# Seven chunk pairs of the token projections as Strassen products, interleaved with blocks of the pair before

## The reference

```python
h = rmsnorm(x, g_mix_pre[l])
proj = h @ w_in[l]                                   # (256, 2048) @ (2048, 7168)
cb, cc, cv, dq, dk, dv, xq = jnp.split(proj, IN_OFFSETS, axis=-1)
y_conv = short_conv_mixer(cb, cc, cv, conv_w[l]) @ w_conv_out[l]
y_diff = diff_attention(dq, dk, dv, ...) @ w_diff_out[l]
y_cross = memory_cross_attention(xq, rmsnorm(mem, g_mem[l]), w_mem_kv[l]) @ w_cross_out[l]
```

## Time and profile before

| | |
|---|---|
| median of 3 runs | 1637.32 us (1637.16 to 1637.5) |
| the profiled execution | 1637.66 us, span 1635.8 us |
| PE, PEld busy | 1624.0 us (99%), 1338.5 us (82%) |
| DVE, ACT busy | 1090.9 us (67%), 858.3 us (52%) |
| DMA | 346.75 MB, mean 212 GB/s |

### The profile page before, as it was taken

The page is one execution under the profiler, slowest core; times in us unless marked ns, Lnnn a source line. Parts: engine busy times, 40 slices in busy tenths (PEclk is TensorE's granted clock), DMA queues, the critical chain, the costliest instruction groups (busy, mean ns, idle before and its releaser), DMA issues.

```text
span 1635.8 us, 21990 instructions
## 1 busy us (share of the span) xinstructions
PE 1624.0 (99%) x7225; PEld 1338.5 (82%) x7225; DVE 1090.9 (67%) x1463; ACT 858.3 (52%) x1080; POOL 54.8 (3%) x117
## 2 busy tenths in 40 slices
PE   9999999999999999999999999999999999999998
PEld 7888888888888888888888888888888888877886
DVE  5664565655566566666665756777766777789886
ACT  6744444444444444444444656666666565555553
POOL 2500000000000000000000000000000000000000
PEclk9999999999999999999999999999999999999999
DMA  8877666777665766676666476777777767665564
GB/s 282 279 223 216 196 183 190 228 215 218 188 208 190 239 216 200 200 235 210 221 222 223 133 224 209 217 219 220 219 216 218 221 204 227 216 203 200 192 206 155
DMA packets 207787, 346.75 MB, mean 212 GB/s; under 512 B 28952, under 2 KB 52329, under 8 KB 207209
## 3 DMA queue, kind: packets, MB, share of 16 engines
q1 hardware_dynamic: 201033, 342.48, 67.2%
q0 software_dynamic: 2048, 2.10, 0.4%
q10 hardware_dynamic: 4640, 1.33, 0.3%
HBM read 318.02 MB, written 2.10 MB: 196 GB/s over the span
## 4 chain that ended last, share of the span: by engine, by line
PE 96%; DVE 2%; DMA 0%; ACT 0%; issue 0%; SPq 0%; POOL 0%; DVEq 0%; ACTq 0%; POOLq 0%
PE PS L1725 24%; PE PS L1727 24%; PE PS L1726 24%; PE PS L1973 3%; PE PS L1974 3%; PE PS L1972 3%; PE PS L1857 3%; PE PS L1859 3%; PE PS L1858 3%; PE PS L1957 1%; PE PS L1959 1%; PE PS L1958 1%; DVE w_lo L1586 1%; PE PS L1893 1%; PE PS L1895 1%; PE PS L1894 1%
## 5 line engine op out<-in xcount | busy, mean ns | idle before, releaser
L1112 DVE TENSOR_TENSOR w_lo<-raw,w_hi 128x1024 fp32r<-128x1024 f32 x479 | 583.1, 1224 | 453.6 <-ACT w_hi L676 452.4
L676 ACT ACTIVATE w_hi<-raw 128x1024 fp32r<-128x1024 f32 x479 | 504.9, 1059 | 496.4 <-PE PS L1727 431.3
L1725 PE MATMUL PS<-w_hi,hT_hi 128*128 128x512 f32 x1504 | 587.7, 391 | 0.0
L1727 PE MATMUL PS<-w_hi,hT_lo 128*128 128x512 f32 x1504 | 585.2, 389 | 0.0
L1726 PE MATMUL PS<-w_lo,hT_hi 128*128 128x512 f32 x1504 | 585.1, 389 | 0.0
L1725 PEld LDWEIGHTS PS<-w_hi,hT_hi 128*128 128x128 f32 x1504 | 282.4, 188 | 61.2 <-issue 2.7
L1727 PEld LDWEIGHTS PS<-w_hi,hT_lo 128*128 128x128 f32 x1504 | 282.4, 188 | 58.5
L1726 PEld LDWEIGHTS PS<-w_lo,hT_hi 128*128 128x128 f32 x1504 | 282.4, 188 | 58.3
L1586 DVE TENSOR_TENSOR w_lo<-raw,w_hi 128x1024 fp32r<-128x1024 f32 x81 | 98.1, 1221 | 28.1 <-ACT w_hi L1030 26.9
L1030 ACT ACTIVATE w_hi<-raw 128x1024 fp32r<-128x1024 f32 x81 | 84.8, 1057 | 59.8 <-PE PS L1974 38.2
L1972 PE MATMUL PS<-w_hi,act_hi 128*128 128x512 f32 x240 | 93.8, 391 | 1.9 <-DVE w_lo L1586 1.9
(11 more groups left out here) (243 smaller groups left out, 1637.7 us busy)
## 6 DMA issues: line engine op xcount, KB each, us to landing
raw<-in_w_up_dram SPq DMA_DIRECT2D x176, 512.0 KB, 4.0
raw<-in_w_in_dram SPq DMA_DIRECT2D x112, 512.0 KB, 4.2
raw<-in_w_gate_dram SPq DMA_DIRECT2D x96, 512.0 KB, 4.6
raw<-in_w_down_dram SPq DMA_DIRECT2D x88, 512.0 KB, 4.4
raw<-in_w_mem_kv_dram SPq DMA_DIRECT2D x32, 512.0 KB, 5.8
raw<-in_w_o_dram SPq DMA_DIRECT2D x32, 512.0 KB, 4.2
up_moved<-up_stage SPq DMA_DIRECT2D x352, 32.0 KB, 2.8
raw<-in_w_conv_out_dram SPq DMA_DIRECT2D x16, 512.0 KB, 3.7
```

The source lines that it names most:

```text
L676: nc.scalar.activation(w_hi[i % RING][:], raw[i % RING][:], ACT.Copy).then_inc(hi_ready, inc)
L1112: nc.vector.tensor_tensor(w_lo[i % RING][:], raw[i % RING][:], w_hi[i % RING][:].bitcast(F32), ALU.subtract).then_inc(lo_ready, inc)
L1725: nc.tensor.matmul(o, a_hi, b_hi, start=first, stop=False)
L1727: last = nc.tensor.matmul(o, a_lo, b_hi, start=False, stop=last_k)
```

## The change

For every even chunk c from 4 to 16 (`PAIRS`) the chunks c and c+1 form a pair. Their blocks 0 and 1 (the first four K tiles) are a matrix of four weight blocks: `b11` and `b21` of chunk c, `B12` and `B22` of chunk c+1. With the four token blocks (two token tiles by two pairs of K tiles) they are computed as seven products by Strassen's scheme (Winograd's form) in place of eight. A product is one weight operand by one token tile: 6 matmuls.

- A group has 11 units (`G_UNITS`), numbered 0 to 10 in the text: products are units 0, 2, 4, 5, 7, 8 and 10; units 1, 3, 6 and 9 are the blocks 4, 5, 6 and 7 of chunk c-1. After the group come blocks 2 to 7 of chunk c, then blocks 2 and 3 of chunk c+1, then the next group.
- Units take the place of blocks in the rings of `w_hi` and `w_lo` (4 deep). The raw ring carries only `b11`, `b21` and ordinary blocks; `B12` and `B22` are loaded into side buffers (`side_load`), where DVE also builds the four weight differences (`difference`, L1515, semaphore `p_sums`).
- Four sums of token blocks are made once (`token_sums`), with their own split `T_hi`, `T_lo`.
- Two partial results that several outputs share are carried by ACT copies (L978 from bank to bank, L987 into `side_q`, semaphore `p_seed`) and two DVE adds per group into PSUM (L1550, L1557, `p_folds`).
- The side work of the blocks that a group passes is called between its units (`after(k)`), and SP's small DMAs stand between other loads (`crossing`, `odd_squares`). An odd chunk uses banks 2 and 3 or 4 and 5 in turn.
- The later stages keep their instructions; their ring indices are rotated.

```diff
+    PAIRS = range(4, NP, 2)
+    G_UNITS = 11
+    N_BR = NP * CB + 3 * len(PAIRS)
+    RING_LOADS = NP * CB - 2 * len(PAIRS)
...
+        ODD = {1: (2, 3), 5: (4,), 7: (5,), 8: (6,), 9: (7,)}
+        THIRD = {1: (4,), 3: (5,), 6: (6,), 9: (7,)}
...
+        def p_passed(c, u):
+
+            if u == G_UNITS - 1:
+                return [(c, 0), (c, 1)]
+            return [(c - 1, i) for i in (THIRD if c == PAIRS[0] else ODD).get(u, ())]
...
+            for c in PAIRS:
+                proj_load(c, 0)
+                if c > PAIRS[0]:
+                    odd_squares(c - 3, 2)
+                proj_load(c - 1, 4)
+                crossing(c - 1, 4)
+                if c > PAIRS[0]:
+                    odd_squares(c - 3, 3)
+                proj_load(c - 1, 5)
+                crossing(c - 1, 5)
+                odd_squares(c - 2, 0)
+                proj_load(c, 1)
+                odd_squares(c - 2, 1)
+                proj_load(c - 1, 6)
+                odd_squares(c - 2, 2)
+                proj_load(c - 1, 7)
+                odd_squares(c - 2, 3)
+                for i in range(2, CB):
+                    proj_load(c, i)
+                    crossing(c, i)
+                    if i in (5, 6) and c + 2 in PAIRS:
+                        side_load(c + 2, i - 5)
+                for i in (2, 3):
+                    proj_load(c + 1, i)
+                    odd_squares(c - 1, i - 2)
...
+            def proj_group(c):      # ACT
+                proj_split(c, 0)
+                if g:
+                    after_projection(c - 2)
+                proj_split(c - 1, 4)
+                after(1)
+                proj_hi(u + 2, E, (p_sums, 4 * g + 1))
+                proj_split(c - 1, 5)
+                after(3)
+                act.wait_ge(block_done, u + 1)
+                nc.scalar.activation(p_bank(c)[:, 0, :], p_bank(c)[:, 1, :], ACT.Copy).then_inc(p_seed, 1)
+                proj_hi(u + 4, E, (p_sums, 4 * g + 3))
...
+            def proj_group(c):      # DVE
+                proj_split(c, 0)
...
+                difference(E, B12, b11)
+                proj_split(c - 1, 4)
+                after(1)
...
+                difference(B12, B22, B12)
+                proj_lo(u + 2, E)
+                dve.wait_ge(lo_ready, u + 3)
+                difference(E, B22, E)
+                proj_split(c - 1, 5)
+                after(3)
+                proj_lo(u + 4, E)
...
+                difference(E, b21, E)
+                proj_split(c, 1)
+                after(5)
+                proj_split(c - 1, 6)
+                after(6)
+                proj_lo(u + 7, B12)
+                after(7)
+                dve.wait_ge(block_done, u + 5)
+                dve.wait_ge(p_seed, 2 * g + 2)
+                nc.vector.tensor_tensor(p_bank(c + 1)[:, 0, :], p_bank(c)[:, 1, :], q5[:], ALU.add).then_inc(p_folds, 1)
...
+            def proj_product(u, o, hi, lo, start=False):
+
+                pe.wait_ge(lo_ready, u + 1)
+                for k in range(KB):
+                    b_hi, b_lo = hi_p[u % RING][:, k, :], lo_p[u % RING][:, k, :]
+                    nc.tensor.matmul(o, hi[:, k, :], b_hi, start=start and k == 0, stop=False, skip_group_check=not start)
+                    nc.tensor.matmul(o, hi[:, k, :], b_lo, start=False, stop=False, skip_group_check=not start)
+                    last = nc.tensor.matmul(o, lo[:, k, :], b_hi, start=False, stop=k == KB - 1, skip_group_check=not start)
+                last.then_inc(block_done, 1)
```

More of the change, by code:

```diff
@@ L757, in _, with proj_hi, proj_split @@
                 prepare_plain(pair)
-            for c, (name, half) in enumerate(proj):
+            def proj_hi(u, src, landed=None):
+                if landed is not None:
+                    act.wait_ge(*landed)
+                if u >= RING:
+                    act.wait_ge(block_done, u - RING + 1)
+                nc.scalar.activation(hi_p[u % RING][:], src[:], ACT.Copy).then_inc(hi_ready, 1)
+            def proj_split(c, i):
+                k = p_at[c, i]
+                proj_hi(p_unit[c, i], raw_p[k % RING], (raw_in_p[k % RING], 16 * (k // RING + 1)))
@@ L759, in _ @@
+            for c in range(3):
                 for i in range(CB):
                     if c or i >= PLAIN:
[L761 to L768, removed]
@@ L813, in _ @@
[L813 to L821 removed]
+                        proj_split(c, i)
@@ new lines, in _ @@
+                    proj_step(c, i)
+            for i in range(4):
+                proj_split(3, i)
+                proj_step(3, i)
+            for c in PAIRS:
+                proj_group(c)
+                for i in range(2, CB):
+                    proj_split(c, i)
+                    proj_step(c, i)
+                proj_split(c + 1, 2)
+                proj_step(c + 1, 0)
+                proj_step(c + 1, 1)
+                proj_split(c + 1, 3)
+            for i in range(4, CB):
+                proj_split(NP - 1, i)
+                if i == 4:
+                    after_projection(NP - 2)
+                    proj_step(NP - 1, 2)
+                    proj_step(NP - 1, 3)
+                proj_step(NP - 1, i)
@@ L1809, in _ @@
[L1809 to L1819 removed]
+                        proj_multiply(c, i)
```

618 lines of the change are left out of this document (421 added, 197 removed).

## The result

The changed kernel takes 1648.29 us (median of 5 executions, 1644.43 to 1649.01) against 1637.49 for the kernel before (5 executions, 1637.16 to 1638.15) on the same chip: a ratio of 1.0061, 95% interval 1.005 to 1.0072. The forecast was 1642.0. The executions of the kernel before lie within 1 us of each other, those of the changed one within 4.6, and they go by the mean granted clock: 1644.43 at 0.998, 1645.8 at 0.997, 1648.29 at 0.996, 1648.67 and 1649.01 at 0.995. The profiled one is that of 1645.8 us.

A forecast was written before the change was run, and what follows sets the result against it. PE, busy 99% of the span, was taken to set the end. Matmuls -9.3, waits +2.3 (group 10), +6.9 (group 12), +4.8 (groups 6, 14, 16) gave +4.7 us: forecast 1642.0 us, range 1635 to 1649.

The forecast's parts named there:

- -9.3 for 41 matmuls: Projections: 42 matmuls fewer, one seeding matmul more, each worth 0.227 us on PE's path, saving 9.3 us.
- PE busy about 9 us less: Sign expected in the new profile: PE's busy time in matmuls falls by about 9 us.
- Groups 6, 14, 16: SP behind the squares: SP's nine slots of squares and loads delay block 6's load; PE stands 1.6 us in each group, 4.8 in all.
- L: Lead of unit 1 of a group: how long before PE needs that unit its split is ready.
- Group 10: 2.3: Convolution work between units 1 and 6 takes 16.4 us, PE needs unit 6 after 9.5; lead 4.6, PE stands 2.3.
- The string: Groups 10 and 12: turn, taps, high halves, splits and transposes in a row, from unit 1's split to unit 6's, 16.4 us.
- Group 12: 6.9 forecast: Same convolution work, but copies also wait for SP's 23 slots; lead about 0, PE stands 6.9 us at units 2, 3, 6.
- The lead of 0.9 at block 4 of chunk 10: Before group 12: squares written 0.9 us before PE begins that block, 3.2 in steady stream less 2.3 from group 10.
- rival A: SP's queue does not bind, only 2 x 2.3 us of convolution waits remain: -4.7 us, 1632.6 us, faster; chance 0.16.
- At nothing: Costed at zero: ACT's extra copies (2 x 0.6 us a group), the token sums at chunk 3, ring rotation and later stages.
- rival E: Clock falls to 1.2 GHz in group 12's waits for the rest of that group: 10 us more, 1652; chance 0.05.
- D: Lateness is handed on from group to group, all later leads zero: 1649 us; chance 0.13.

The follow-up runs named there:

- squares from POOL: Changed kernel with the small DMAs of the projections' squares issued by POOL instead of SP: 1637.03 us, ratio 1.0000.
- late taps: Changed kernel, groups 10 and 12: ACT's first convolution tap moved from unit 1 to 7, DVE's eight taps from unit 5 to 9: 1641.33 us.
- both edits: Changed kernel with the squares' DMAs on POOL and the convolution taps moved to units 7 and 9: 1628.90 us, ratio 0.9949.
- taking only the tap away: Changed kernel with squares' DMAs on POOL and only ACT's first convolution tap moved, from unit 1 to unit 3: 1636.27 us, ratio 0.9993.
- the waits filled: Changed kernel with 40 scratch matmuls put in front of PE's waits in groups 6, 10, 12, 14 and 16: 1642.20 us.

## Why the prediction was right in its terms and short in its time

| us of PE's wait in group | 4 | 6 | 8 | 10 | 12 | 14 | 16 | sum |
|---|---|---|---|---|---|---|---|---|
| forecast | 0 | 1.6 | 0 | 2.3 | 6.9 | 1.6 | 1.6 | 14.0 |
| changed kernel | 0 | 2.4 | 0 | 2.3 | 5.1 | 1.2 | 1.4 | 12.5 |
| squares from POOL | 0 | 0 | 0 | 2.1 | 3.5 | 0.2 | 0 | 5.9 |
| late taps | 0 | 1.8 | 0 | 0 | 3.0 | 2.7 | 2.0 | 9.5 |
| both | 0 | 0 | 0 | 0 | 0 | 0.2 | 0 | 0.2 |

**Slower, and where.** Right: the waits come at the five groups named, for the releaser named, none at 4 and 8, none for a fold. With the 0.27 us that each wait costs beyond its bracket they are 14.9 us, against 14.0. That these are so close is partly luck: the sum had no term for stopping and starting (9 x 0.27 = 2.4), and group 12 was put 1.8 too high.

**-9.3 for 41 matmuls.** Right, shown by the version with both edits. The 5.4 us that the issue gap of the Trainium skill ("TensorE: Matmul & The Clock Gate", section "Back-to-back issue gap") would give is ruled out here: 8.4 us came. The sign "PE busy about 9 us less" did not come in the changed kernel (4.1 less): matmuls at 1.2 GHz are longer, about 3.1 us in two stretches, and the time beyond the brackets counts as busy, 9 x 0.27 = 2.4. In the version with both edits, with one short wait and no stretch, it is 9.7.

**Groups 6, 14, 16: SP behind the squares.** Right, 4.8 forecast and 5.1 measured, gone with the squares on POOL. SP's queue in group 6:

```profile
130.77 2.41 SPq L492 DMA_DIRECT2D proj_moved<-proj_stage  x4
133.23 0.58 SPq L528 DMA_DIRECT2D raw<-in_w_in_dram  x1
133.85 3.42 SPq L492 DMA_DIRECT2D proj_moved<-proj_stage  x4
137.32 0.58 SPq L528 DMA_DIRECT2D raw<-in_w_in_dram  x1
```

It starts when the turn of the chunk before is done (130.70) and issues block 6 at 137.32; the 5.5 us of nine slots were 6.5. ACT has the block only after this wait:

```profile
141.59 1.06 ACT L887 ACTIVATE w_hi<-raw 128x1024 fp32r<-128x1024 f32 x1 [2.54 <-DMA raw<-in_w_in_dram]
```

From the end of unit 1's split (129.37) to that of unit 6 (143.90) are 14.5 us, forecast 13.4; PE began unit 1 at 131.52, so L was 2.2, forecast 2.3. That SP works without a pause was wrong: it stood from 124.50 to 130.77, waiting for that turn, and was late all the same.

**Group 10: 2.3.** Right to the tenth, partly by luck. The string from the end of one split to that of the other (221.05 to 237.79) was 16.7 us against 16.4, and PE began unit 1 at 225.85, so L was 4.8 against 4.6 (the forecast's own terms sum to 4.7): two misses of 0.2 to 0.3 that cancel. Link by link the string is the forecast's, the first tap with 1.62 us against 1.59. The maximum of the scores, 0.8 us on DVE, was not in the forecast; it lies beside the tap and costs nothing there, since DVE still waits for ACT behind it:

```profile
225.30 1.23 DVE L1409 TENSOR_TENSOR w_lo<-side,w_hi 128x1024 fp32r<-128x1024 f32 x1 [0.81 <-ACT w_hi L887]
```

That is why taking only the tap away gained so little: DVE's own work filled the gap.

**Group 12: 6.9 forecast, 5.1 measured.** The pieces fell at units 2, 3 and 6 as said; the string was right, 16.5 us (276.15 to 292.68):

```profile
272.67 1.27 ACT L853 ACTIVATE proj_stage<-PS,r_x 128x512 f32<-128x512 f32 x2 [3.45 <-DMA proj_moved<-proj_stage]
```

```profile
274.92 1.23 DVE L1409 TENSOR_TENSOR w_lo<-raw,w_hi 128x1024 fp32r<-128x1024 f32 x1 [3.30 <-ACT w_hi L887]
...
291.50 1.18 DVE L1409 TENSOR_TENSOR w_lo<-raw,w_hi 128x1024 fp32r<-128x1024 f32 x1
```

The copies did wait 3.45 us for the last square. The term that was mis-sized is L. The split of unit 1 ended at 276.15 and PE began unit 1 at 277.42, so L was 1.3, not 0. It was the chain through SP's queue that was put too long. From the first square's issue (256.87) to that split's end it took 19.3 us, forecast 20.6: the copies began at 272.67, 1.3 us after SP had issued the last square, where the forecast added the median landing time of 3.1. The lead of 0.9 at block 4 of chunk 10 was nearly right (1.2: squares written at 256.84, PE at that block at 258.00), but not for its reason. The forecast had taken it as group 10's lateness handed on. But DVE stood 3.24 us in between, waiting for PE's scores, and wrote the squares behind their maximum:

```profile
252.75 0.69 DVE L1473 TENSOR_REDUCE top<-PS 128x2 f32<-128x512 f32 x1 [3.24 <-PE PS L2124]
254.69 2.15 DVE L1369 SCALAR_TENSOR_TENSOR proj_stage<-PS,r_x,cc_sb 128x128 f32<-128x128 f32 x8
```

So L = 1.2 + 19.4 - 19.3 = 1.3. At the other end, L "up to 4.6" was too high: with the queue out of the way it is 3.1 (split ready at 271.09, unit 1 begun at 274.15). The 4.6 of group 10 holds a step of scores, 1.73 us of PE in which the others catch up, and there is none in the stretch before group 12 (so 2.9); the last of four starts at 250.82:

```profile
220.04 1.89 PE L2124 MATMUL PS<-mkT,xqT 128*128 128x256 f32 x8
250.82 1.89 PE L2124 MATMUL PS<-mkT,xqT 128*128 128x256 f32 x8
```

So rival A would have been about 1637 (measured 1637.03, with waits of 5.9, their stopping and one stretch at 1.2 GHz), not 1632.6: even with SP out of the way the change as ordered gains nothing.

**At nothing:** ACT's copies, shown by doubling them in the version with both edits. The token sums and the ring rotation were not tried by themselves, but that version contains them and is within 0.4 us of the sum, so they cost no more than tenths.

**The step that failed: the clock.** The sum had no term for what follows a wait, neither for the clock nor for the 2.4 us of stopping and starting. I treated it as rival E, with a chance of 0.05 and a price of 10 us for one place, and reasoned that the opening of the kernel, where PE is idle 1.6 us of 10, keeps 1.00. In fact waits of 2.3 and 3.1 us, right after a stretch of full work, sufficed, and in other runs waits from 2.1 us up; each fall costs 1.5 us, not 10, but there are several in an execution, an estimated 4.6 us in the median run. The rule of the Trainium skill cited at E ("TensorE: Matmul & The Clock Gate", section "HAM oscillation — how this bites in real kernels") names the mechanism; the trace agrees with it in kind, and its price is the 1.55 us above. Without the clock the terms as measured give 1637.5 - 9.3 + 14.9 = 1643.1, and 1642.2 was measured with the waits filled; the forecast's 1642.0 would have been right to about 1 us. That the measured 1648.3 still lies under the forecast's upper end of 1649 is luck: that end stood for D, every lead lost, and the leads were 2.2, 4.8 and 1.3 us in groups 6, 10 and 12.

## What to carry to other kernels

Saving work on the bound engine pays only if the order of the others is rebuilt with it. With units of half the length PE comes sooner to the block that a string of side work or a full queue holds back (9.5 us for a string of 16.5 here). In this kernel two moves in the order (small DMAs to an idle engine's queue, eight taps a few units later) turned +10.8 us into -8.4. Price a wait of PE of more than 2 us at its length, plus 0.3 for stopping and starting, plus 1.5 for the clock, which fell behind 11 of 14 such waits here. When executions that used to agree within 1 us spread over 5, look at the granted clock right behind the waits before looking for anything else.

## What the runs showed of the hardware

- A single wait of PE of 2.1 to 3.9 us was followed in 11 cases of 14 by a granted clock of 0.5 for a little over 3 us, which cost about 1.55 us; equal waits of 2.60 us went both ways in one execution. Behind none of up to 1.97 us did the clock fall in a profiled execution.
- A wait costs PE about 0.27 us beyond what the view shows: 0.16 before the first matmul and 0.11 between the first and the second.
- POOL issues a small DMA of 32 KB in 0.49 us (16 in 7.87 us), SP one in 0.60; on POOL the median time to landing was 4.0 us against 3.1 on SP.
